# Two blocks with a gated linear recurrence: the order of three vector steps in the recurrence

## The reference

```python
def step(state, xs):
    qc, lfc, kc, vc = xs
    b = jnp.cumsum(lfc, axis=2)
    o_inter = jnp.einsum('bhtk,bhkv->bhtv', qc * jnp.exp(b), state)
    diff = b[:, :, :, None, :] - b[:, :, None, :, :]
    decay = jnp.exp(jnp.where(causal, diff, -jnp.inf))
    attn = jnp.einsum('bhtk,bhsk,bhtsk->bhts', qc, kc, decay)
    o_intra = jnp.einsum('bhts,bhsv->bhtv', attn, vc)
    ...
    return new_state, o_inter + o_intra
...
o = rms_norm(o, hgrn_norm_w[l]) * jax.nn.silu(heads(g_h, HGRN_HEAD_V))
```

## Time and profile before

| | |
|---|---|
| median of three runs | 2010.11 us |
| the profiled execution | 2011.31 us |
| its span, first to last instruction | 2009.2 us |
| PE busy | 1946.7 us (97%) |
| DVE busy | 1414.2 us (70%) |
| POOL busy | 949.4 us (47%) |
| ACT busy | 837.7 us (42%) |
| mean granted clock of TensorE | 0.988 |

### The profile page before, as it was taken

One profiled execution on the slowest core, in us unless ns is written; L12 is line 12 of the kernel. 1 busy time (PEld: TensorE's weight loads), 2 busy tenths in 40 slices (PEclk: granted clock), 3 DMA queues, 4 the chain that ended last, 5 costly groups with the idle time before them and its releaser, 6 DMA issues.

```text
span 2009.2 us, 28818 instructions
## 1 busy us (share of the span) xinstructions
PE 1946.7 (97%) x10693; PEld 1588.1 (79%) x10693; DVE 1414.2 (70%) x1824; ACT 837.7 (42%) x1337; POOL 949.4 (47%) x548
## 2 busy tenths in 40 slices
PE   7999999999999999999999899898999999999997
PEld 7878778788887768878888578777888888888886
DVE  7799999878747655786231586898865665657977
ACT  6545544355520034562300576566332332334453
POOL 1444455433334478743453200946745555544553
PEclk8999999999999999999999899999999999999998
DMA  9223222211122253232110200232432332356344
GB/s 295 68 84 116 71 76 104 94 31 42 43 64 64 63 176 119 84 137 86 52 52 0 84 2 3 73 126 85 126 110 78 125 103 85 121 196 221 101 141 162
DMA packets 179503, 194.01 MB, mean 97 GB/s; under 512 B 9863, under 2 KB 122968, under 8 KB 179418
## 3 DMA queue, kind: packets, MB, share of 16 engines
q1 hardware_dynamic: 172996, 178.53, 28.0%
q10 hardware_dynamic: 6422, 14.37, 2.0%
HBM read 151.71 MB, written 41.16 MB: 96 GB/s over the span
## 4 chain that ended last, share of the span: by engine, by line
PE 79%; DVE 13%; ACT 4%; issue 3%; POOL 1%; ACTq 0%; DVEq 0%; POOLq 0%
PE psum L1575 7%; PE psum L1577 7%; PE psum L1576 7%; PE psum L1009 6%; PE psum L1011 6%; PE psum L1010 6%; PE psum L1678 3%; PE psum L1680 3%; PE psum L1679 3%; PE psum L1033 3%; PE psum L1032 3%; PE psum L1031 3%; PE psum L1336 2%; PE psum L1338 2%; PE psum L1337 2%
## 5 line engine op out<-in xcount | busy, mean ns | idle before, releaser
L801 POOL TENSOR_TENSOR w_hi<-w_raw,ones_r 128x1024 fp32r<-128x1024 f32 x60 | 153.9, 2565 | 448.1 <-PE psum L1011 324.9
L1009 PE MATMUL psum<-h_hi,w_hi 128*128 128x512 f32 x704 | 282.2, 401 | 0.0
L1011 PE MATMUL psum<-h_hi,w_lo 128*128 128x512 f32 x704 | 275.0, 391 | 0.0
L1010 PE MATMUL psum<-h_lo,w_hi 128*128 128x512 f32 x704 | 274.8, 390 | 0.0
L804 POOL TENSOR_TENSOR w_lo<-w_raw,w_hi 128x1024 fp32r<-128x1024 f32 x60 | 166.6, 2777 | 4.7
L1710 ACT ACTIVATE arena<-psum 128x1024 f32<-128x1024 f32 (+7 forms) x103 | 80.6, 787 | 207.8 <-PE psum L1011 108.3
L1011 PEld LDWEIGHTS psum<-h_hi,w_lo 128*128 128x128 f32 x704 | 132.4, 188 | 28.2
L1009 PEld LDWEIGHTS psum<-h_hi,w_hi 128*128 128x128 f32 x704 | 132.6, 188 | 27.6 <-issue 0.7
L1010 PEld LDWEIGHTS psum<-h_lo,w_hi 128*128 128x128 f32 x704 | 132.7, 188 | 26.4 <-issue 0.7
L1678 PE MATMUL psum<-w_hi,h_hi 128*128 128x512 f32 x308 | 121.1, 393 | 3.4 <-DVE h_lo L3349 3.4
L999 POOL TENSOR_TENSOR w_lo<-arena,w_hi 128x512 fp32r<-128x512 f32 x61 | 86.7, 1425 | 75.4 <-ACT w_hi L1710 75.4
(11 more groups left out here) (496 smaller groups left out, 5233.8 us busy)
## 6 DMA issues: line engine op xcount, KB each, us to landing
w_raw<-w_in SPq DMA_DIRECT2D x64, 512.0 KB, 4.0
act_op<-arena SPq DMA_DIRECT2D x77, 256.0 KB, 2.3
arena<-act_op SPq DMA_DIRECT2D x77, 256.0 KB, 2.7
w_raw<-w_gate SPq DMA_DIRECT2D x22, 512.0 KB, 4.1
w_raw<-w_up SPq DMA_DIRECT2D x22, 512.0 KB, 5.3
arena<-ada_w SPq DMA_DIRECT2D x16, 512.0 KB, 7.2
arena<-w_out SPq DMA_DIRECT2D x16, 512.0 KB, 6.0
out_T<-arena SPq DMA_DIRECT2D x16, 512.0 KB, 5.8
```

Source lines behind the costliest of these rows:

```text
L1009: pe.matmul(o, wh, xh, start=(k == 0), stop=False)
L1010: pe.matmul(o, wh, xl, start=False, stop=False)
L1011: return pe.matmul(o, wl, xh, start=False, stop=(k == KT - 1))
```

## The change

In `spans`, `back_3(h - 1)` moves ahead of the wait for `eb_done` and the queries' product. In head 0 the decay sums of head 1 move from inside `f` to behind picks 3 and 4. The other heads' decay sums stay where they were. Lines below the edit move by two.

```diff
@@ -2682,10 +2682,10 @@
                     squares_lo(h - 1)
                 base_q(h)
                 span_kq(h, 0)
+                if not (type(h) is int and h == 0):
+                    back_3(h - 1)
                 dve.wait_ge(eb_done, h + 1)
                 TT(qe, qe, qq, ALU.mult).then_inc(qe_done, 1)
-                if not (type(h) is int and h == 0):
-                    back_3(h - 1)
                 span_kq(h, 1)
@@ -2702,6 +2702,8 @@
                 f()
                 pick(h, 3, at)
                 pick(h, 4, at)
+                if h == 0:
+                    decay_sums(1)
@@ -2723,7 +2725,8 @@
                 def next_f():
                     gate_f(it)
-                    decay_sums(it)
+                    if it > 1:
+                        decay_sums(it)
                 spans(it - 1, lambda: gate_g(it), next_f)
```

## The result

Over sixteen runs each, the changed kernel took 2013.37 us (median, 2009.11 to 2018.77) and the kernel before 2009.41 us (2006.06 to 2013.19). The ratio is 1.0021, with a 95% interval of 1.0014 to 1.0028: slower by 4.2 us (3 to 6). The prediction said 6.3 us slower, inside a range of -9 to +13; in absolute times 2016.4 us against the 2013.4 measured.

The account below looks back on a forecast made before the run. PE was taken as the bound, with DVE setting the pace in heads 1 to 4; 16 us of gains, taken back by POOL's collisions, left +5.8 us at head 2 and +6.3 at head 5: 2016.4 us, range 2001 to 2023.

Parts of the forecast that it names:

- step 3: Head 1: POOL's train holds DVE's four operations through `sq_lo`; PE waits some 11 us, head 2 opens 5.8 us later.
- The half-clock term: Head 1: a half-clock stretch of PE behind its wait for `sq_lo`, counted as 1.7 us.
- Steps 1 and 2: Heads 2 to 4: about 2.7 of 2.83 us waits go, three times; head 0: 5.7 us in all go.
- Step 4, head 2: In head 2 POOL holds three of eight decay sums; PE waits 5.0 us, head 3 opens at 278.9.
- Step 4, head 3: In head 3 the decay sums are held again, PE waiting 5.0 us; period 64.6 us, head 4 opens at 343.5.
- (a): Rival, heads 0 and 2 to 4: DVE keeps what it gains; faster, 2002.5 or 2006.3 us; chance 0.23.
- (c): Rival, whole recurrence: all of PE's stalls go, 17.0 us faster, 1993.1 us; chance 0.07.
- (b): Rival: DVE holds the lock through head 1, `sq_lo` in time; within 3 us of 2010.1; chance 0.16.

Follow-up runs that it names:

- e3: The changed kernel with POOL's train of four in heads 1 to 4 also waiting for the squares' low part; 2007.8 us, 0.9992 to the kernel before.
- e8: The changed kernel with only POOL's pair ahead of an opening also waiting for the decay sums; 2014.0 us, 1.0017 to the kernel before.
- e7: The changed kernel with POOL's sixteen tile sums cut from 1024 elements to 8; 1993.4 us, 0.9920 to the kernel before.
- e10: The kernel before with only POOL's train of four waiting for the squares' low part; 2004.5 us, 0.9968 to the kernel before.
- e1: The kernel before with only `back_3` moved ahead of the queries' product, head 0's decay sums unmoved; 2012.4 us, 1.0011 to the kernel before.

## Why the prediction was right, and where it was off

*The mechanism* of step 3 was right in order and in size. Expected: train at 152.8, `sq_lo` ready at 165.2 or 163.0, a wait of some 11 us, head 2 at 214.9. Measured: 152.5, 164.85, 3.0 + 8.2 us, 215.55. e3 shows that POOL was the cause. The half-clock term was near: I counted 1.7 us lost, and the lower clock covered the 3.7 us of work from the wait's end (164.9) to 168.6, about 1.9 us lost.

*Steps 1 and 2* were right: the waits of 2.83 us went, in heads 2 and 4 L2712 runs behind a held operation (in heads 1 and 3 it waits 2.40 and 6.32 us for ACT's root, still in time for PE), head 1 opens at 143.5, L2578 starts at 146.19 (expected 146.3).

*Step 4, head 2*: expected a wait of 5.0 us at the opening of head 3 and the opening at 278.9; measured 4.35 and 278.80.

*Step 4, head 3, is the term that failed.* I had the same collision again and a period of 64.6 us; measured 60.9 (339.72 - 278.80), with no wait at the opening of head 4. The eight sums took 5.91 us, not 9.07:

```profile
330.25 5.91 DVE L2571 TENSOR_TENSOR_SCAN arena<-ones_r,arena 128x128 f32<-128x128 f32 x8 [1.13 <-ACT arena L1846]
```

```profile
333.25 2.63 POOL L801 TENSOR_TENSOR w_hi<-w_raw,ones_r 128x1024 fp32r<-128x1024 f32 x1 [1.74 <-PE psum L1011]
```

What I left out is the half clock behind the wait of 4.35 us. It puts PE some 3 us back, so POOL's pair comes 3.0 us behind the start of the sums, when most are done; in head 2 it came 0.2 us behind. The train of four comes late in the same way, at 290.73, when DVE has one short product left before it waits for ACT's root, so none of the products ahead of the norm's first step is held. So a slower PE protects DVE here, as I read it. No run tests it alone, but e3 fits: there the half clock behind a like wait (4.23 us at the opening of head 3) ended at 274.7, after 3.4 us, POOL's pair came 0.2 us behind the start of the sums again, and PE waited 4.37 us at the opening of head 4.

```profile
324.46 9.08 DVE L2573 TENSOR_TENSOR_SCAN arena<-ones_r,arena 128x128 f32<-128x128 f32 x8 [1.13 <-ACT arena L1848]
```

With 60.9 in place of 64.6 the sum is +2.6, and the traces have +2.0 at the opening of head 5.

*The runs.* +4.2 us in the median is more than the +2.0 of the traces at head 5, and the spans of the two profiled executions differ by only 0.2. Behind 1,100 us the changed kernel's gets back 1.1 and 0.7 us: the clock is at its lower level from 1124.5 to 1138.0 in the trace of before and from 1127.8 to 1137.9 in that of the change, and from 1988.1 to 1994.8 against 1991.4 to 1994.6. Both profiled executions of the change took less than the median of its runs (2013.4 and 2015.4), that of before more than its own (2011.3 against 2009.4). What the upper group of its runs does differently, in the recurrence or behind it, stays open, since no trace of one was had; a course like e8's, with 64.2 us in head 3, is one possibility. The stated 6.3 us are 2.1 us from the measured 4.2, the corrected 2.6 are 1.6 from it; that the kernel came out slower is the merit of step 3, and step 4 has no part in the nearness of the number.

*The rivals.* (a) and (c) needed DVE to keep its gain, and the trains to stay out of its way; e7 is what (c) would look like from head 2 on, at 58.1 us a head, and takes the tile sums away for it. Of the signs named for (a), periods under 61 us, heads 3 and 4 show one (60.9 and 59.3), but behind a head 1 of 72.1 and a head 2 of 63.3. (b) did not happen: at 152.67 DVE was held at once. Why POOL waited 4.68 us at 107.25 wasn't tried.

## What to carry to other kernels

Where two engines exclude each other from a memory port, an operation's price depends on when it meets the other, so price a reordering by the collisions that it moves and not by the wait that it removes: here 13.6 us of waits were removed and 16.0 came back, most of them in front of another semaphore. Look at what the waiting engine releases when it stops waiting; here PE, some 6 us earlier than before, released POOL's work into the one stretch of DVE's that PE would need next. And before reordering the victim, hold back the aggressor: two waits on POOL gave 9 us, and none of the three orders of DVE's that were tried without them was faster than before.

## What the runs showed that I had not expected

A hold that moves the start of POOL's train by only 0.5 us in heads 3 and 4 and 1.4 in head 2, from the time in which L2671 runs to 0.16 us behind its end, takes 2.2 us off PE's wait in each of these heads, because one more operation of DVE's begins ahead of POOL; the runs are 6 us faster for it (e10, 0.9968).

And the length of a wait did not tell what it did to the clock. Of the three waits of 2.83 us of before, the clock was at its lower level behind the first (3.4 us) and stayed at the full one behind the other two; behind the 3.50 us of e10 it stayed there too. In e1 the wait of 4.24 us was followed by 3.4 us at the lower level and the shorter one of 3.15 by 6.8:

```profile
208.70:215.40 6.70, 5.54 (x26) 5.55 (x27) 5.43 (x7) 1.40 (x2) 0.00 (x0) 0.50 0.00 0
...
335.00:338.30 3.30, 3.30 (x18) 3.30 (x17) 2.14 (x4) 1.06 (x1) 0.00 (x0) 0.50 0.00 0
```
